# Two-block transformer on one core: last items of the first mixers and stage borders in another order, both tiles' FFN turns in one place, pool means on fewer columns

## The chip, the cores and the metric

The program runs on one core of a Trainium2 chip. Time is the device time of one execution in microseconds (us); lower is better. The engines are named as the profile names them: PE is TensorE (PEld its weight loads), DVE is VectorE, ACT is ScalarE, POOL is GpSimd, SP is SyncE, which here only issues the transfers of weights.

## What is computed

The input x has 256 rows of 1024 columns in float32. Two blocks run one after the other, each of two layers, and each layer is a chain of stages of one form: `x = x + norm(f(norm(x)))`. There are ten stages in all:

```
for l in (0, 1):   # first block
    x = x + rmsnorm(mixer1(rmsnorm(x)))          # four attention kinds, concatenated, @ w_out
    x = x + rmsnorm((silu(h @ w_gate) * (h @ w_up)) @ w_down),  h = rmsnorm(x)
for l in (0, 1):   # second block
    x = x + 0.5 * rms_norm(swiglu(rms_norm(x)))
    x = x + rms_norm(mixer2(rms_norm(x)))        # projections, trailing means, causal convolution, gates
    x = x + 0.5 * rms_norm(swiglu(rms_norm(x)))
```

The inner width of each of the six feed-forward nets (FFN) is 2816. mixer1 has four kinds of attention with four heads of 64 each (moba, fox, mla, dilated), causal within the 256 rows. mixer2 subtracts p from its trailing mean over windows of 2, 4, 8 and 16 rows, one window for each group of 256 columns:

```
def trailing_mean(u, win):
    cs = jnp.cumsum(u, axis=1)
    cs_shift = jnp.pad(cs, ((0, 0), (win, 0), (0, 0)))[:, :s]
    return (cs - cs_shift) / count[None, :, None]     # count = min(row + 1, win)
```

## The kernel before

**Tiles and units.** The rows are two tiles of 128, t = 0 and t = 1. The weights come as units of 128 x 2048 float32 (1 MB) in a fixed row, numbered g. SP loads unit g into one of three buffers `raw`, ACT copies it, rounded to fp32r, into one of four buffers `whi` (two copies of 128x1024, `hi_a` and `hi_b`, L667), and DVE writes the rest `raw - whi` into `wlo` (two halves, `lo`, L1117). A buffer of `whi` comes free when PE has done unit g - 4 for tile 1. `refill(freed)` is the splitting of unit freed + 4. The activations are split the same way (`a_hi`/`a_lo`, `b_hi`/`b_lo`, `f_hi`/`f_lo`). Every product with weights is three matmuls (`three`, L1770 to L1772): high by high, high by low, low by high. One step of PE is one unit for one tile, 12 matmuls of 512 columns; in the FFN row k is step k of tile 0 and then step k - 2 of tile 1.

**Order.** Each engine's order is written out by hand, in loops of Python that are unrolled; the engines meet by semaphores. PE names the sources of waits: `split_done` (weights), `alo` (activations), `fm` (the gated product of the FFN), `o_lo` (a mixer item's heads), `pfree` (a PSUM bank evicted).

**FFN.** In `swiglu` on PE, `gate_up` makes one block j of 256 columns of gate and up, ACT takes the silu (L761), DVE multiplies (L1218, `mult`). `turn_f` (L1825, its transposes L1829) turns the 128x256 product by two PE transposes into `Tp`, ACT and DVE split it into `f_hi` and `f_lo` (L771, L1224), and `down` multiplies it with unit `dn_unit(j)`. There are 11 blocks j for each tile, so 22 pairs of transposes in each FFN.

**First mixer.** It has eight items, M0 to F1 (a kind and a tile). For each: turn q and k (L1945), scores (L1954), mask and maxima on DVE, exponentials on ACT (L871), `turn_p` (L1966), copies of the turned probabilities out of PSUM (`p_out`: the first half by ACT, L882, the second by DVE, L1458), values (L1978), `normalise` (L1471), `turn_heads` (L1984), and `heads_hi`/`heads_lo` (L888, L1479), before `out_part` multiplies the item with its unit of w_out. The last is F1. PE does `turn_p(F1)`, then `out_part(1, OUT_L, L1)`; between the two halves of that (`middle`) stand `values(F1)` and `turn_x_both(0, s+1)`, and behind it `turn_heads(F1)` and `out_part(1, OUT_F, F1)`.

**Borders.** `boundary` on ACT (L732) and DVE (L1185) is what happens between two stages: sums of squares of y (L715), the residual (L1161), x turned by PE (L1785), gained (L1177), and split again (L721, L1182), with three units' splitting in between. It has hooks for work of the first mixer. `first_eviction` is the first work of the next stage. `silu_table` (L755) makes ACT load the table of the silu.

**Start of a first mixer on DVE** (`mixing1`, L1481 on): the latents of tile 0 are normalised, unit b + 4 is split (b is the mixer's first unit; b + 4 is `MV`, the values of moba, which PE takes in `values_chunk`), `rotate_moba` (L1373 to L1382) evicts and rotates q and k, `latents_lo` (L1357, L1359) waits for ACT's copy of the turned latents. In layer 0 the two halves of unit b + 4 stand before `rotate_moba` and behind `latents_lo`, in layer 1 both stand before `rotate_moba`. In layer 1 ACT's `latents_hi` (L837, L839) follows `latents(1, l)` (L829, L832), which waits for the half of unit b + 1 of tile 1.

**Pool means.** `band` holds for each window a 128 x 384 matrix; `pool_means` (L2220 on) multiplies tile 0's rows with its columns 0 to 255 and tile 1's rows with columns 256 to 383, for two column blocks m of each of the four windows.

## Time and profile before

| | us |
|---|---|
| median of 3 runs | 1834.16 (1832.75 to 1835.46) |
| the profiled execution, its own time | 1835.75 |
| its span, first to last instruction | 1834.0 |
| PE busy | 1808.9 (99%) |
| DVE busy | 1110.6 (61%) |
| ACT busy | 911.4 (50%) |
| mean granted clock of PE | 0.998 |

The times of instructions are us from the start of the span. A matmul's duration overlaps the next one's, so the distance from start to start tells what one costs. "[0.93 <-DVE ...]" behind a row is idle time of the engine ahead of that instruction and what ended it. PEclk is the granted clock of TensorE as a share of full speed.

### The profile page before, as it was taken

Reading aid. Unit: us, or ns where it says so; the run is one execution under the profiler, and the core shown is the slowest. Engines: PE = TensorE matmul, PEld = TensorE weight load, DVE = VectorE, ACT = ScalarE, POOL = GpSimd, SP = SyncE. Lnnn points to the kernel's source line nnn. Section 1 sums busy time; section 2 is a strip of 40 time slices with the busy share of each in tenths; the row PEclk is TensorE's granted clock in tenths of the full one; section 3 lists DMA queues with packets and bytes.
Section 4 is the critical chain, followed back from the end, with each engine's and each line's share of the span. In section 5 each row is a group of like instructions: output and inputs, shape, how many; then the busy total and the mean of one; then the engine's idle time right before and its main releaser. Section 6 shows DMA issues by size and latency. Waiting matters only on the chain.

```text
span 1834.0 us, 21875 instructions
## 1 busy us (share of the span) xinstructions
PE 1808.9 (99%) x8663; PEld 1506.9 (82%) x8663; DVE 1110.6 (61%) x1444; ACT 911.4 (50%) x1382; POOL 86.4 (5%) x209
## 2 busy tenths in 40 slices
PE   7999999999999999999999999999999999999998
PEld 6888888888788888888888888888888888888887
DVE  7766655776655575556566765556555666675554
ACT  6555444655544454445455444445444545454443
POOL 4001000200000010001000000001000100010000
PEclk9999999999999999999999999999999999999999
DMA  7434555633455565556555565556555655556552
GB/s 233 138 115 159 185 184 170 197 119 115 162 191 191 190 213 189 184 184 207 168 182 192 170 195 191 188 184 218 184 184 187 208 178 173 195 165 202 184 183 92
DMA packets 221462, 327.80 MB, mean 179 GB/s; under 512 B 10576, under 2 KB 156528, under 8 KB 221104
## 3 DMA queue, kind: packets, MB, share of 16 engines
q1 hardware_dynamic: 218880, 318.64, 53.1%
q0 software_dynamic: 2176, 7.75, 1.4%
q8 instruction: 69, 1.13, 0.3%
q14 instruction: 33, 0.27, 0.0%
q10 hardware_dynamic: 304, 0.01, 0.0%
HBM read 325.31 MB, written 1.05 MB: 178 GB/s over the span
## 4 chain that ended last, share of the span: by engine, by line
PE 96%; ACT 1%; POOL 1%; DVE 1%; issue 1%; DMA 0%; DVEq 0%; POOLq 0%; ACTq 0%
PE Dp L1770 17%; PE Dp L1772 17%; PE Dp L1771 17%; PE Gp L1772 12%; PE Gp L1770 12%; PE Gp L1771 12%; PE Tp L1829 2%; PE Gp L1954 1%; PE Tp L1945 1%; PE Dp L1978 1%; PE Tp L1785 0%; PE Gp L1785 0%; PE Tp L1978 0%; DVE wlo L1117 0%; ACT whi L667 0%
## 5 line engine op out<-in xcount | busy, mean ns | idle before, releaser
L1117 DVE TENSOR_TENSOR wlo<-raw,whi 128x1024 fp32r<-128x1024 f32 (+1 forms) x608 | 715.2, 1214 | 359.2 <-ACT whi L667 359.0
L667 ACT ACTIVATE whi<-raw 128x1024 fp32r<-128x1024 f32 (+1 forms) x608 | 606.5, 1045 | 292.1 <-PE Dp L1772 160.1
L1770 PE MATMUL Gp<-whi,a_hi 128*128 128x512 f32 x960 | 380.1, 396 | 0.0
L1772 PE MATMUL Gp<-whi,a_lo 128*128 128x512 f32 x960 | 374.6, 390 | 0.0
L1771 PE MATMUL Gp<-wlo,a_hi 128*128 128x512 f32 x960 | 373.9, 389 | 0.0
L1770 PE MATMUL Dp<-whi,a_hi 128*128 128x512 f32 (+2 forms) x768 | 294.0, 383 | 4.9 <-DVE wlo L1117 3.2
L1772 PE MATMUL Dp<-whi,a_lo 128*128 128x512 f32 (+2 forms) x768 | 287.9, 375 | 0.0
L1771 PE MATMUL Dp<-wlo,a_hi 128*128 128x512 f32 (+2 forms) x768 | 287.6, 375 | 0.0
L1772 PEld LDWEIGHTS Gp<-whi,a_lo 128*128 128x128 f32 x960 | 180.1, 188 | 38.6
L1771 PEld LDWEIGHTS Gp<-wlo,a_hi 128*128 128x128 f32 x960 | 180.5, 188 | 35.9
L1770 PEld LDWEIGHTS Gp<-whi,a_hi 128*128 128x128 f32 x960 | 180.3, 188 | 35.5
L1770 PE MATMUL Dp<-whi,f_hi 128*128 128x512 f32 x504 | 202.1, 401 | 0.0
L1772 PE MATMUL Dp<-whi,f_lo 128*128 128x512 f32 x504 | 197.7, 392 | 0.0
L1771 PE MATMUL Dp<-wlo,f_hi 128*128 128x512 f32 x504 | 196.5, 390 | 0.0
L1770 PEld LDWEIGHTS Dp<-whi,a_hi 128*128 128x128 f32 x768 | 145.2, 189 | 30.4 <-DVE wlo L1117 4.1
L1772 PEld LDWEIGHTS Dp<-whi,a_lo 128*128 128x128 f32 x768 | 145.0, 189 | 25.5
L1771 PEld LDWEIGHTS Dp<-wlo,a_hi 128*128 128x128 f32 x768 | 145.3, 189 | 23.4
L761 ACT ACTIVATE inner<-Gp,st 128x256 f32<-128x256 f32 x120 | 57.0, 475 | 215.7 <-PE Gp L1772 215.7
L771 ACT ACTIVATE f_hi<-Tp 128x256 fp32r<-128x256 f32 x126 | 48.3, 384 | 189.8 <-PE Tp L1829 189.8
L1218 DVE SCALAR_TENSOR_TENSOR inner<-Gp,st,inner 128x256 f32<-128x256 f32 x120 | 57.7, 481 | 130.5 <-ACT inner L761 130.5
L1224 DVE TENSOR_TENSOR f_lo<-Tp,f_hi 128x256 fp32r<-128x256 f32 x126 | 53.1, 422 | 113.3 <-ACT f_hi L771 113.2
L1772 PEld LDWEIGHTS Dp<-whi,f_lo 128*128 128x128 f32 x504 | 94.6, 188 | 20.6
(261 smaller groups left out, 1649.7 us busy)
## 6 DMA issues: line engine op xcount, KB each, us to landing
raw<-in_ffn_w_gate_up SPq DMA_DIRECT2D x176, 512.0 KB, 4.7
raw<-in_w_in SPq DMA_DIRECT2D x132, 512.0 KB, 4.6
raw<-in_ffn_w_down SPq DMA_DIRECT2D x88, 512.0 KB, 4.4
raw<-in_w_gate SPq DMA_DIRECT2D x44, 512.0 KB, 3.8
raw<-in_w_up SPq DMA_DIRECT2D x44, 512.0 KB, 4.8
raw<-in_w_down SPq DMA_DIRECT2D x44, 512.0 KB, 4.3
raw<-in_w_out SPq DMA_DIRECT2D x16, 512.0 KB, 4.0
raw<-in_w_pool_out SPq DMA_DIRECT2D x16, 512.0 KB, 4.2
```

Source lines behind the costliest of these rows:

```text
L667: return nc.scalar.activation(whi[g % W][0:rows, c0:c0 + n], raw[g % R][0:rows, c0:c0 + n], ACT.Copy).then_inc(hi_done, 1)
L761: nc.scalar.activation(gate[:, t, :], gu_bank(t, j)[:, 0:FC], ACT.Silu, scale=rsx[:, t:t + 1]).then_inc(silu[t], 1)
L771: nc.scalar.activation(f_buf(j, t)[0], T(t, 256).rearrange("p (k s) -> p k s", k=2), ACT.Copy).then_inc(fhi[t], 1)
L1117: return V.tensor_tensor(wlo[g % W][0:rows, c0:c0 + n], raw[g % R][0:rows, c0:c0 + n], whi[g % W][0:rows, c0:c0 + n].bitcast(F32), ALU.sub ...
L1218: V.scalar_tensor_tensor(out=ffn[:, t, :], in0=gu_bank(t, j)[:, FC:2 * FC], scalar=rsx[:, t:t + 1], in1=gate[:, t, :], op0=ALU.mult, op1=A ...
L1224: V.tensor_tensor(lo_, T(t, 256).rearrange("p (k s) -> p k s", k=2), hi_.bitcast(F32), ALU.subtract).then_inc(flo[t], 1)
L1770: mm(o, hi, wh, start=start, stop=False, skip_group_check=True)
L1771: mm(o, hi, wl, start=False, stop=False, skip_group_check=True)
L1772: return mm(o, lo, wh, start=False, stop=stop, skip_group_check=True)
L1829: ins = nc.tensor.transpose(T(t)[:, P * k:P * k + P], ffn[:, t, P * k:P * k + P], ident[:, :])
L1945: ins = nc.tensor.transpose(T(e, 512, dq)[:, P * h:P * h + P], of(kind, t, h), ident[:, :])
L1954: ins = mm(score_view(n)[:, h, :], qT[0:dq, h, :], kT[0:dq, h, 0:nk], start=True, stop=True)
```

## The change

Five edits, all of order but for the last:

1. First mixer, item F1 (both layers): ACT's `p_out(F1)` moves from behind the table load and `refill(last - 2)` to right behind the exponentials. PE's `turn_heads(F1)` moves into `middle`, behind `turn_x_both`. DVE's `heads_lo(F1)` moves between the two `gained` of tile 0.
2. All nine borders: ACT's splitting of unit last + 4 (`refill(last)`) stood behind `first_eviction`; now `hi_a` stands ahead of `turned_hi(1, 0)` and `hi_b` between the two `turned_hi` of tile 1. DVE's part stays.
3. Layer 1's first mixer on DVE: the order of layer 0 is used, so the second half of unit b + 4 moves behind `rotate_moba` and `latents_lo`.
4. FFN: `turn_f(1, j - 1)` moves from its own step to behind `turn_f(0, j)`, ten times in each of six FFNs; ACT's and DVE's splits move with it.
5. Pool means: tile 0's rows are multiplied with the first 128 + window columns of the band (130, 132, 136 and 144) in place of 256.

```
@@ scalar: boundary
                     hi_b(last - 1 + W)
                     square_x(0, s + 1)
+                    if last + W <= LAST:
+                        hi_a(last + W)
                     turned_hi(1, 0, s + 1)
+                    if last + W <= LAST:
+                        hi_b(last + W)
                     turned_hi(1, 1, s + 1)
                     first_eviction()
-                    refill(last)
                     square_x(1, s + 1)
@@ scalar: ffn_step (vector: the same with mult and f_low)
-                elif i == 2:
-                    f_hi_out(t, F, 0)
+                elif (t, i) == (0, 2):
+                    f_hi_out(0, F, 0)
...
-                elif i % 3 == 1 and 4 <= i <= 31:
-                    f_hi_out(t, F, i // 3)
+                elif t == 0 and i % 3 == 1 and 4 <= i <= 31:
+                    f_hi_out(0, F, i // 3)
+                    f_hi_out(1, F, i // 3 - 1)
+                elif (t, i) == (1, NFFN - 2):
+                    f_hi_out(1, F, NJ - 1)
@@ scalar: hooks of mixing1
                     heads_hi(L1, l)
                     softmax(F1, l)
+                    p_out(F1, l)
                     silu_table()
 
                 def after_refill():
-                    p_out(F1, l)
                     heads_hi(F1, l)
@@ vector: boundary
                 if s + 1 < STAGES:
                     gained(0, 0, s + 1)
+                    between_gained()
                     gained(0, 1, s + 1)
@@ vector: mixing1
-                if l:
-                    refill(b + 0)
-                    rotate_moba(0, l)
-                    latents_lo(0, l)
-                else:
-                    lo(b + W, 0)
-                    rotate_moba(0, l)
-                    latents_lo(0, l)
-                    lo(b + W, 1)
+                lo(b + W, 0)
+                rotate_moba(0, l)
+                latents_lo(0, l)
+                lo(b + W, 1)
...
-                def after_gained():
+                def between_gained():
                     heads_lo(F1, l)
@@ tensor: swiglu, step
-                        if i == 2:
-                            turn_f(t, 0)
+                        if (t, i) == (0, 2):
+                            turn_f(0, 0)
...
-                        if (t, i) != (1, NFFN - 2):
-                            turn_f(t, i // 3)
+                        if t == 0:
+                            turn_f(0, i // 3)
+
+                            turn_f(1, i // 3 - 1)
@@ tensor: mixing1
                     turn_x_both(0, s + 1)
 
+                    turn_heads(F1)
+
                 out_part(1, OUT_L, L1, False, False, middle)
-
-                turn_heads(F1)
                 out_part(1, OUT_F, F1, False, True)
@@ tensor: pool_means
-                        mm(bank, rows_of(ZB, 0, c)[:, o:o + P], band[:, g, 0:S], start=True, stop=True)
+                        reach = P + WINDOWS[g]
+                        mm(bank[:, 0:reach], rows_of(ZB, 0, c)[:, o:o + P], band[:, g, 0:reach], start=True, stop=False,
+                           skip_group_check=True)
```

Where the instructions stand now is seen at three places. The lines of code differ by a few between the two kernels: L882, L755 and L721 of before are L888, L758 and L721 of the change. First, ACT at the end of layer 0's first mixer, before (L871 are the exponentials of F1, `loaded2` is the transfer of a unit):

```order
L871 ACTIVATE Z,sm<-Z,sm 128x256 x3
L755 ACT_TABLE_LOAD
L755 ACTIVATE st<-st 128x1
L667 ACTIVATE whi<-raw 128x1024 [waits done1,loaded2]
L667 ACTIVATE whi<-raw 128x1024
L882 ACTIVATE Z<-Gp 128x512 [waits p_turned]
L888 ACTIVATE b_hi<-Gp 128x2x128 [waits o_turned]
L721 ACTIVATE a_hi<-stage 128x4x128 [waits gn0] x2
```

and ACT at the same place in the change:

```order
L877 ACTIVATE Z,sm<-Z,sm 128x256 x3
L888 ACTIVATE Z<-Gp 128x512 [waits p_turned]
L758 ACT_TABLE_LOAD
L758 ACTIVATE st<-st 128x1
L667 ACTIVATE whi<-raw 128x1024 [waits done1,loaded2]
L667 ACTIVATE whi<-raw 128x1024
L894 ACTIVATE b_hi<-Gp 128x2x128 [waits o_turned]
L721 ACTIVATE a_hi<-stage 128x4x128 [waits gn0] x2
```

The copy of the turned probabilities has passed the table load, the dummy silu and the two halves of a unit.

Second, DVE at the start of layer 1's first mixer, before (L1117 are halves of unit b + 4 and then of b + 5, L1338 ends the rotation of the latents' key):

```order
L1338 TENSOR_TENSOR Z<-Z 128x4x16
L1117 TENSOR_TENSOR wlo<-raw,whi 128x1024 [waits hi_done] x2
L1373 SCALAR_TENSOR_TENSOR stage<-Dp,st,sinh 128x512 [waits done0]
L1375 SCALAR_TENSOR_TENSOR Z<-Dp,st,cosh 128x512
L1381 TENSOR_TENSOR Z<-Z,stage 128x8x32 [waits pfree0,rope_m0]
L1382 TENSOR_TENSOR Z<-Z,stage 128x8x32
L1357 TENSOR_TENSOR b_lo<-Tp,b_hi 96x2x128 [waits lhi0]
L1359 TENSOR_TENSOR b_lo<-Tp,b_hi 128x128
L1395 TENSOR_TENSOR st<-Z,bfor 128x8 [waits gmla_in,lat_out1,lat_out0]
```

and DVE there in the change:

```order
L1348 TENSOR_TENSOR Z<-Z 128x4x16
L1123 TENSOR_TENSOR wlo<-raw,whi 128x1024 [waits hi_done]
L1383 SCALAR_TENSOR_TENSOR stage<-Dp,st,sinh 128x512 [waits done0]
L1385 SCALAR_TENSOR_TENSOR Z<-Dp,st,cosh 128x512
L1391 TENSOR_TENSOR Z<-Z,stage 128x8x32 [waits pfree0,rope_m0]
L1392 TENSOR_TENSOR Z<-Z,stage 128x8x32
L1367 TENSOR_TENSOR b_lo<-Tp,b_hi 96x2x128 [waits lhi0]
L1369 TENSOR_TENSOR b_lo<-Tp,b_hi 128x128
L1123 TENSOR_TENSOR wlo<-raw,whi 128x1024 [waits hi_done]
L1405 TENSOR_TENSOR st<-Z,bfor 128x8 [waits gmla_in,lat_out1,lat_out0]
```

The second half of unit b + 4 has moved behind six instructions, two of which wait on ACT's `lhi0`.

Third, PE in a row of the FFN, before, the step `down` of tile 0 with what stands ahead of and behind it (the twelve matmuls of the step are cut to their first and last):

```order
L1829 MATMUL Tp<-ident,inner 128x128 [waits fm1]
L1829 MATMUL Tp<-ident,inner 128x128
L1770 MATMUL Dp<-whi,f_hi 128x512 [waits split_done,flo0]
...
L1772 MATMUL Dp<-whi,f_lo 128x512
L1829 MATMUL Tp<-ident,inner 128x128 [waits fm0]
L1829 MATMUL Tp<-ident,inner 128x128
L1770 MATMUL Gp<-whi,a_hi 128x512 [waits fm1]
```

and PE there in the change:

```order
L1775 MATMUL Dp<-whi,f_hi 128x512 [waits split_done,flo0]
...
L1777 MATMUL Dp<-whi,f_lo 128x512
L1834 MATMUL Tp<-ident,inner 128x128 [waits fm0]
L1834 MATMUL Tp<-ident,inner 128x128
L1834 MATMUL Tp<-ident,inner 128x128 [waits fm1]
L1834 MATMUL Tp<-ident,inner 128x128
L1775 MATMUL Gp<-whi,a_hi 128x512 [waits fm1]
```

Tile 1's pair of transposes has moved one step later and stands behind tile 0's.

## Rows read from the trace of the kernel before

**Rows 1.** The page, busy time of each engine and its share of the span.
```profile
PE 1808.9 (99%) x8663; PEld 1506.9 (82%) x8663; DVE 1110.6 (61%) x1444; ACT 911.4 (50%) x1382; POOL 86.4 (5%) x209
```

**Rows 2.** Waits of PE, the largest in the body: us in total, times, longest.
```profile
PE Tp L1978 <- ACT Z L882: 2.8, 2, 1.4
```

**Rows 3.** Timeline, end of layer 0's first mixer: start, duration, instruction.
```profile
132.71 1.28 ACT L755 ACT_TABLE_LOAD   x1
133.87 0.69 DVE L1458 COPY Z<-Gp 128x512 f32<-128x512 f32 x1 [0.95 <-PE Gp L1966]
134.11 1.99 ACT L667 ACTIVATE whi<-raw 128x1024 fp32r<-128x1024 f32 x2
134.83 0.40 PE L1772 MATMUL Dp<-whi,b_lo 128*128 128x512 f32 x1
136.63 2.00 PE L1978 MATMUL Tp<-Z 128*128 128x64 f32 x16 [1.41 <-ACT Z L882]
...
142.76 0.38 ACT L888 ACTIVATE b_hi<-Gp 128x256 fp32r<-128x256 f32 x1 [6.18 <-PE Gp L1984]
143.65 0.50 PE L1770 MATMUL Dp<-whi,b_hi 128*128 128x512 f32 x1 [0.93 <-DVE b_lo L1479]
```

**Rows 4.** Stretches: length, busy PE, PEld, DVE, ACT, POOL, PEclk, DMA.
```profile
135.30:138.70 3.40, 2.07 (x19) 2.07 (x20) 0.03 (x1) 1.28 (x2) 0.00 (x0) 1.00 0.00 0
138.70:142.10 3.40, 3.40 (x13) 2.92 (x12) 1.77 (x3) 0.00 (x0) 0.00 (x0) 0.50 0.00 0
456.10:459.50 3.40, 3.40 (x14) 3.03 (x14) 1.81 (x3) 0.00 (x0) 0.00 (x0) 0.50 0.00 0
96.40:98.13 1.73, 1.73 (x17) 1.73 (x16) 0.44 (x3) 1.47 (x2) 0.00 (x0) 1.00 1.02 407
123.30:126.70 3.40, 3.40 (x25) 3.19 (x24) 2.07 (x2) 2.00 (x2) 0.00 (x0) 1.00 0.35 121
```

**Rows 5.** Timeline of PE, steady step and a pair of transposes (501.53), layer 1's FFN.
```profile
501.30 0.39 PE L1772 MATMUL Dp<-whi,f_lo 128*128 128x512 f32 x1
...
504.29 0.39 PE L1772 MATMUL Gp<-whi,a_lo 128*128 128x512 f32 x1
...
508.60 0.39 PE L1770 MATMUL Gp<-whi,a_hi 128*128 128x512 f32 x1
...
510.87 0.39 PE L1771 MATMUL Gp<-wlo,a_hi 128*128 128x512 f32 x1
```

**Rows 6.** Timeline of PE around four transposes in a run (L1966 at 47.46).
```profile
47.23 0.39 PE L1772 MATMUL Dp<-whi,a_lo 128*128 128x512 f32 x1
...
50.44 0.40 PE L1772 MATMUL Dp<-whi,a_lo 128*128 128x512 f32 x1
```

**Rows 7.** Timeline of PE in the pool means, first window, layer 0.
```profile
872.23 0.60 PE L2229 MATMUL Tp<-band,Z 128*128 128x256 f32 x2
872.67 0.38 PE L2230 MATMUL Tp<-band,Z 128*128 128x128 f32 x2
872.89 0.60 PE L2229 MATMUL Tp<-band,Z 128*128 128x256 f32 x2
```

**Rows 8.** Timeline, border into layer 1's first mixer and its start.
```profile
340.76 0.63 ACT L721 ACTIVATE a_hi<-stage 128x512 fp32r<-128x512 f32 x1 [1.10 <-DVE stage L1177]
343.61 2.36 DVE L1117 TENSOR_TENSOR wlo<-raw,whi 128x1024 fp32r<-128x1024 f32 x2 [1.49 <-ACT whi L667]
344.89 0.50 PE L1770 MATMUL Dp<-whi,a_hi 128*128 128x512 f32 x1 [1.08 <-DVE wlo L1117]
349.69 0.38 PE L1929 MATMUL Tp<-ident,Z 128*96 128x128 f32 x2
350.81 0.39 PE L1770 MATMUL Dp<-whi,a_hi 128*128 128x256 f32 x1 [0.63 <-DVE Z L1375]
352.09 0.28 DVE L1359 TENSOR_TENSOR b_lo<-Tp,b_hi 128x128 fp32r<-128x128 f32 x1
353.77 1.03 PE L1945 MATMUL Tp<-ident,Z 128*64 128x128 f32 x8
```

More of the change, by code:

```diff
@@ L1183, in turned_lo, with boundary @@
                                 ).then_inc(alo[t], 1)
-            def boundary(s, last, after_scaled, after_residual, after_gained, first_eviction):
+            def boundary(s, last, after_scaled, after_residual, between_gained, after_gained, first_eviction):
                 scaled(0, 0, s)
@@ L1229, in ffn_step @@
                     mult(t, F, 0)
-                elif i == 2:
-                    f_low(t, F, 0)
+                elif (t, i) == (0, 2):
+                    f_low(0, F, 0)
                 elif i % 3 == 0 and 3 <= i <= 30:
                     mult(t, F, i // 3)
-                elif i % 3 == 1 and 4 <= i <= 31:
-                    f_low(t, F, i // 3)
+                elif t == 0 and i % 3 == 1 and 4 <= i <= 31:
+                    f_low(0, F, i // 3)
+                    f_low(1, F, i // 3 - 1)
+                elif (t, i) == (1, NFFN - 2):
+                    f_low(1, F, NJ - 1)
             def swiglu(F, g0, between=None):
@@ L1248, in end_of_ffn @@
             def end_of_ffn(s, F, g0, first_eviction):
-                boundary(s, g0 + NFFN - 1, nothing, lambda: ffn_step(1, F, NFFN - 3),
+                boundary(s, g0 + NFFN - 1, nothing, lambda: ffn_step(1, F, NFFN - 3), nothing,
                          lambda: ffn_step(1, F, NFFN - 2), first_eviction)
@@ L1581, in after_residual @@
                     normalise(F1, l)
-                def after_gained():
+                def between_gained():
                     heads_lo(F1, l)
-                return after_scaled, after_residual, after_gained
+                return after_scaled, after_residual, between_gained, nothing
             def v_eviction(t, c, l):
@@ L1760, in _ @@
                 g0 = mixer2(l) + 37
-                boundary(s_mix2(l), g0 - 1, nothing, nothing, nothing, lambda: mult(0, f_22(l), 0))
+                boundary(s_mix2(l), g0 - 1, nothing, nothing, nothing, nothing, lambda: mult(0, f_22(l), 0))
                 swiglu(f_22(l), g0)
```

## The prediction

> **What bounds the kernel.** The page first: PE is busy 1808.9 of 1834.0 us, no other engine over 61% [rows 1]. So the time is PE's own work, plus its idle time (25 us, part of it in the start-up, which the change leaves alone), plus what the granted clock takes. A change of order can win only (a) a wait of PE, (b) a stretch at half clock, (c) the small losses at the seams between kinds of matmul; taking columns away wins (d) their streaming time.
>
> The waits of PE come next. The largest in the body is that of `values(F1)` for ACT's copy: 2.8 us in two waits, one for each layer of the first mixer [rows 2]. The timeline shows what stands there [rows 3]: PE has its last matmul at 134.83 and could go on at 135.06 (matmuls start 0.227 us apart: 2.27 for ten, 508.60 to 510.87 [rows 5]). It starts at 136.63, because ACT first loads a table (1.28) and splits a unit (1.99). Then comes a stretch in which PE is busy with only 2.07 of 3.40 us, and behind it the granted clock is 0.50 from 138.7 to 142.1, and in the same way from 456.1 to 459.5 in the other layer [rows 4]; 0.50 is the lower of TensorE's two levels, 1.2 GHz. Last, PE waits 0.93 for DVE's `heads_lo(F1)` at 143.65.
>
> **Edit 1, item F1.** The copy needs turned probabilities and a free ACT. ACT is free at 132.71; DVE does the other half of the same copy from 133.87 to 134.56 with its order unchanged [rows 3], and ACT's half is released earlier, by the first four transposes. So both halves are done by 134.56, ahead of PE's 135.06: the wait goes whole. From there at full clock: 16 value products 1.73 (96.40 to 98.13 [rows 4]); ten transposes, eight of x and the two of `turn_heads(F1)` that now stand here, at 0.11 each, 1.10 (0.11: see edit 4); the second half of `out_part(L1)`, six matmuls 1.36, and 0.13 for the seam. 135.06 + 1.73 + 1.10 + 1.36 + 0.13 = 139.4 for the first matmul of `out_part(F1)`, where before had 143.65: **4.3 us**. Of this 1.6 is the first wait and up to 1.7 the half clock (3.40 us at half rate do the work of 1.70), and the rest is the wait at 143.65, which is hidden now: the heads' transposes start at 137.7 and are out by 138.3, and from the start of ACT's `heads_hi` to PE it took 0.89 (142.76 to 143.65), so 139.2, with 0.2 in hand. ACT is free for it at 134.1 + 1.28 + 1.99 = 137.4. What is late next: DVE's `gained(0, 1)` now waits behind `heads_lo(F1)`, which moves the border's chain (split, residual, gained) some 0.3 to 0.5 us closer to PE. Ahead of `turn_f(0, 0)` there is almost nothing in hand, so I allow 0.1 of new wait. Two layers: 2 x 4.3 = 8.6, less 0.1.
>
> Bounds: if the clock still falls in both layers, 8.6 - 3.4 = 5.2; if the border gives back 0.5 each, 7.6.
>
> A rule of the skill speaks against the whole of this. The Trainium skill, TensorE: Matmul & The Clock Gate, Part 4, says that PE transposes do not count as busy in the same way as matmuls for the clock; the edit puts ten of them behind 16 small products, 2.8 us without one large matmul. By that rule the clock might fall as before, and the sum would be 3.4 less; by the row the stretch 123.3 to 126.7 is all small products, PE busy throughout, and keeps 1.00. I follow the row, and keep the fall as a rival.
>
> **Edit 2, the borders.** `hi_b` of unit last + 4 goes into a gap of ACT that is 1.10 long (340.76 [rows 8]) and takes 0.99 to 1.05 (half of 1.99 [rows 3]); `hi_a` goes into a longer one ahead. It fits with some 0.05 to spare, so no `turned_hi` comes later: 0. If it did not fit, the first block's product would be late by what is missing. The one gain is at the border into layer 1's mixer: PE's wait of 1.08 for the split of that unit (344.89), with the tail of the matmul before it 1.24, goes, since DVE need not wait for ACT (its 1.49 of idle time at 343.61).
>
> **Edit 3, start of layer 1's mixer.** With `rotate_moba` one half (1.2) and edit 2's gain earlier, the wait of 0.63 at 350.81 (0.8 with the tail) goes as well: 2.0 together. But the second half of unit b + 4 is now behind `latents_lo`, and `values_chunk` needs it after 12 of its 24 matmuls. In before, `latents_lo` ended at 352.37, 2.68 behind the start of the turned latents (349.69), a chain over ACT that follows PE. 349.69 moves to 348.45; `latents_lo` ends at 351.13, the half at 351.13 + 1.18 = 352.3, where PE wants it at 348.8 + 1.5 = 350.3. The new wait is 2.0 and PE goes on at 352.3 with 12 matmuls, 1.5: 353.8 for the next item, where before had 353.77 [rows 8]. **Edits 2 and 3 together: 0**; what the border gives, the moved half takes back. Bounds: -2 (if the half were early) to +0.5.
>
> **Edit 4, the turns.** A pair alone: from 501.30 to 504.29 there are twelve steps of 0.227 (2.72) and the pair, so it costs 0.27 [rows 5]. Four in a run: 47.23 to 50.44 is 3.21, so 0.49 [rows 6]; the two added cost 0.22, 0.11 each. Two pairs apart cost 0.54, together 0.49: 0.05 saved. Ten in each of six FFNs: 60 x 0.05 = **3.0 us**. No engine waits newly: tile 1's split has four steps (11 us) before its `down`. Bounds: 0 if the seam's loss comes once for each bank rather than for each run, 4 by the rounding of the rows (0.01 on each).
>
> **Edit 5, pool means.** Two instructions of 256 columns take 0.44 (872.23 to 872.67), two of 128 take 0.22 (to 872.89) [rows 7]: 0.86 ns a column and instruction. The columns fall by 126, 124, 120 and 112, 482 in sum, in two instructions for each of two blocks and two layers: 482 x 8 x 0.86 ns = **3.3 us**. Bounds: 3.0 to 3.4, since 128 columns already run at the rate of 256.
>
> **Sum.** 8.5 + 0 + 3.0 + 3.3 = 14.8 us. Against the profiled execution's own time: 1835.75 - 14.8 = 1820.9. The median of the runs is 1.6 under that execution and the lowest 3.0; an execution of before that did not fall to half clock would be about 3 lower, and of the change none should fall. So I read the sum from the profiled time, and lean 0.4 toward the median: **1820.5**. A difference of 0.2% (3.7 us) is about what a measurement of this kernel tells from none.
>
> **Rivals.**
> - Half clock stays in both layers: for it the rule above, against it the stretch at 123.3. Then 14.8 - 3.4 = 11.4, 1824 (in one layer, 1822.5). Chance 0.14.
> - The seam's loss is per bank, edit 4 gives nothing: 14.8 - 3.0 = 11.8, 1823.5. For it: the four in rows 6 write one bank, the new four write two. Chance 0.12.
> - Layer 1's half comes early enough or late with more: 1819, or 1822. Chance 0.08.
> - Only the waits that a row names move, and reordering gives back the rest at the border (as for edits 2 and 3, also for edit 1): the columns and half the turns are left, under 5 us, 1830. The change does not do what it says. Chance 0.04.
> - Slower: at the nine borders ACT now stands in `hi_a(last + 4)` before `turned_hi(1, 0)`. If the unit's transfer has not landed, ACT waits, the turned x of tile 1 waits behind it, then the first silu, then PE. It decides from 14.8 / 9 = 1.65 us of wait in each border. Against it: the `whi` that the rows show at this place (134.11) waited for no transfer. At 2 us each it would be 1839. Chance 0.03.
> - The forecast, 1818.5 to 1822.5 by the bounds of edits 1, 4 and 5: 0.59.
>
> The range takes in all but the last two and the far end of the first, where both the clock falls and the turns give nothing (14.8 - 6.4 = 8.4, 1827): 1817 to 1825. Faster by over 0.2%: 0.94; same 0.03; slower 0.03.
>
> The changes of sign come from the last rival (slower) and from half of the one before it with more given back (same).
>
> **What the profile of the changed kernel should show.** No wait of PE at L1978's counterpart, the first `out_part(F1)` matmul near 139.4; no slice with PEclk 0.50 in the two mixers (edit 1 right); a wait of about 2 us of PE for DVE's `wlo` in layer 1's `values_chunk`, inside a run of 256-column matmuls (edit 3 right), none at 344.89's counterpart (edit 2); each FFN shorter by 0.5, no wait of PE in it; the pool means of a window at 0.9 us in place of 1.3. I would be wrong if a new wait stood at each border, or if the stretch behind F1 still ran at 0.50.

## The result, and the profile after

| | before | after |
|---|---|---|
| median, us (lowest to highest) | 1834.81 (1832.75 to 1836.18) | 1820.52 (1820.10 to 1820.59) |
| ratio, 95% interval | | 0.9923 [0.9911, 0.9935] |
| profiled execution, its own time | 1835.75 | 1820.46 |
| its span | 1834.0 | 1818.7 |

The change is faster by 14.3 us in the medians and by 15.3 in the two profiled executions. The forecast was 14.8 against the profiled one and 1820.5 for the time.

The busy line of the page, after. It answers to [rows 1].

```profile
PE 1800.1 (99%) x8663; PEld 1506.4 (83%) x8663; DVE 1103.8 (61%) x1444; ACT 912.9 (50%) x1382; POOL 95.7 (5%) x209
```

PE is busy 8.8 us less, and idle 6.5 us less (18.6, before 25.1). The instruction counts are the same. POOL's are the same instructions too, and take 9.3 us more in all (95.7, before 86.4): in every profile with edit 2 POOL is busy 95.7 to 96.7 us, in every one without it 85.7 to 87.0. Why is not shown; behind the start-up PE waits for POOL nowhere. The waits of PE, after, largest first:

```profile
PE Dp L1775 <- DVE wlo L1123: 3.9, 3, 2.0
...
PE Dp L1775 <- DVE a_lo L1188: 0.9, 1, 0.9
PE Tp L1943 <- DVE st L1419: 0.8, 1, 0.8
PE Dp L1961 <- DVE Z L1431: 0.4, 1, 0.4
PE Tp L1952 <- DVE b_lo L1369: 0.3, 1, 0.3
```

The wait for ACT's copy of F1's probabilities [rows 2] is gone. Of the first row, two waits of 2.2 together lie in the start-up, where before has them too; 1.65 is new. Line numbers have moved: `three` is now L1775 to L1777, `values` L1985, ACT's copy L888.

The timeline at the end of layer 0's first mixer answers to [rows 3].

```profile
133.58 0.60 ACT L888 ACTIVATE Z<-Gp 128x512 f32<-128x512 f32 x1 [0.75 <-PE Gp L1973]
134.02 0.69 DVE L1468 COPY Z<-Gp 128x512 f32<-128x512 f32 x1 [0.95 <-PE Gp L1973]
134.20 1.28 ACT L758 ACT_TABLE_LOAD   x1
134.97 0.40 PE L1777 MATMUL Dp<-whi,b_lo 128*128 128x512 f32 x1
135.21 1.89 PE L1985 MATMUL Tp<-Z 128*128 128x64 f32 x16
135.60 1.99 ACT L667 ACTIVATE whi<-raw 128x1024 fp32r<-128x1024 f32 x2
137.82 0.38 PE L1991 MATMUL Gp<-ident,inner 128*128 128x128 f32 x2
138.24 0.38 ACT L894 ACTIVATE b_hi<-Gp 128x256 fp32r<-128x256 f32 x1 [0.65 <-PE Gp L1991]
138.66 0.42 DVE L1489 TENSOR_TENSOR b_lo<-Gp,b_hi 128x256 fp32r<-128x256 f32 x1 [0.38 <-ACT b_hi L894]
139.43 0.40 PE L1775 MATMUL Dp<-whi,b_hi 128*128 128x512 f32 x1
```

Read it by PE: no row of PE has a bracket, so it has no idle time. ACT's copy is done at 134.18 and DVE's at 134.71, PE takes them at 135.21. `out_part(F1)` starts at 139.43, 4.46 us behind the last matmul of the first half (134.97); in before the same two were 8.82 apart (134.83 and 143.65 [rows 3]). DVE's `b_lo` ends at 139.08, 0.35 ahead of PE.

The stretches that answer to [rows 4], and one in the start-up:

```profile
26.58:29.99 3.41, 3.34 (x8) 2.66 (x9) 2.49 (x9) 2.12 (x8) 2.88 (x6) 0.50 0.72 112
137.00:140.41 3.41, 3.41 (x22) 2.97 (x22) 2.77 (x6) 2.20 (x5) 0.00 (x0) 1.00 0.00 0
450.00:453.41 3.41, 3.41 (x21) 2.93 (x20) 2.91 (x6) 2.19 (x5) 0.00 (x0) 1.00 0.00 0
```

Behind F1 the clock keeps 1.00 in both layers. In this execution it fell once in the start-up, at 26.58, at the end of a wait of 1.97 (PE goes on at 26.65); before has this wait too (1.87), without a fall.

Layer 1's start, DVE and PE, answers to [rows 8]:

```profile
343.81 0.27 PE L1937 MATMUL Tp<-ident,Z 128*128 128x128 f32 x1
344.12 0.38 PE L1775 MATMUL Dp<-whi,a_hi 128*128 128x256 f32 x1
...
346.00 0.28 DVE L1369 TENSOR_TENSOR b_lo<-Tp,b_hi 128x128 fp32r<-128x128 f32 x1
346.19 1.21 DVE L1123 TENSOR_TENSOR wlo<-raw,whi 128x1024 fp32r<-128x1024 f32 x1
...
347.46 0.39 PE L1775 MATMUL Dp<-whi,a_hi 128*128 128x256 f32 x1 [1.65 <-DVE wlo L1123]
349.00 0.27 PE L1952 MATMUL Tp<-ident,Z 128*64 128x128 f32 x1
```

`values_chunk` starts at 344.12 without a bracket. It is not quite free of the rotation: it starts 0.31 behind the transpose ahead of it, where in e9 below, in which the rotation is long done, the same two are 0.02 apart. It then stands still in its middle until the second half of unit b + 4, split from 346.19 on, is done.

Four transposes in a run in an FFN of layer 1 (x4 in one row), then the block of a window's pool means:

```profile
491.90 0.39 PE L1777 MATMUL Dp<-whi,f_lo 128*128 128x512 f32 x1
492.13 0.60 PE L1834 MATMUL Tp<-ident,inner 128*128 128x128 f32 x4
...
495.08 0.39 PE L1777 MATMUL Gp<-whi,a_lo 128*128 128x512 f32 x1
...
861.93 0.39 PE L2237 MATMUL Tp<-band,Z 128*128 128x130 f32 x2
862.16 0.38 PE L2239 MATMUL Tp<-band,Z 128*128 128x128 f32 x2
862.38 0.39 PE L2237 MATMUL Tp<-band,Z 128*128 128x130 f32 x2
```

From 491.90 to 495.08 are 3.18 us: twelve steps of 0.227 and 0.46 for the four. One block of the means takes 0.45 (861.93 to 862.38), before 0.66 [rows 7].

To see where the 15.3 us come from, the same matmul (counted from the start) is looked up in both timelines:

| stretch | before | after | less by |
|---|---|---|---|
| start to the last matmul ahead of values(F1), layer 0 | 134.83 | 134.97 | -0.14 |
| from there to the first matmul behind turn_f(0, 0) | 20.92 | 16.62 | 4.30 |
| on to the border into layer 1's mixer (one FFN) | 184.43 | 183.84 | 0.59 |
| border and start of layer 1, to the next 512-column matmul behind turn_qk(M0) | 14.38 | 14.36 | 0.02 |
| to the last item of layer 1 | 97.69 | 97.69 | 0.00 |
| item F1 of layer 1, with its border | 21.16 | 16.83 | 4.33 |
| the two second mixers | 428.80 | 425.57 | 3.23 |
| the other five FFNs | | | 2.95 |

### The profile page after: what moved, and what is told of

Same layout as the page of the kernel before. It is cut to its first block, busy times and chain, and to the rows that moved or that the text cites. A ratio compares the mean times of both kernels' runs of the same rounds, so it can differ in the third digit from the quotient of the medians.

```text
span 1818.7 us, 21875 instructions
## 1 busy us (share of the span) xinstructions
PE 1800.1 (99%) x8663; PEld 1506.4 (83%) x8663; DVE 1103.8 (61%) x1444; ACT 912.9 (50%) x1382; POOL 95.7 (5%) x209
## 4 chain that ended last, share of the span: by engine, by line
PE 97%; POOL 1%; DVE 1%; issue 0%; ACT 0%; DMA 0%; DVEq 0%; POOLq 0%; ACTq 0%
PE Dp L1775 18%; PE Dp L1777 18%; PE Dp L1776 18%; PE Gp L1775 12%; PE Gp L1777 12%; PE Gp L1776 12%; PE Tp L1834 2%; PE Gp L1961 1%; PE Tp L1952 1%; PE Dp L1985 1%; PE Tp L1790 0%; PE Gp L1973 0%; PE Gp L1790 0%; PE Tp L1985 0%; PE Dp L1961 0%
## 5 line engine op out<-in xcount | busy, mean ns | idle before, releaser
L1775 PE MATMUL Gp<-whi,a_hi 128*128 128x512 f32 x960 | 379.6, 395 | 0.0
L1777 PE MATMUL Gp<-whi,a_lo 128*128 128x512 f32 x960 | 374.3, 390 | 0.0
L1775 PE MATMUL Dp<-whi,a_hi 128*128 128x512 f32 (+2 forms) x768 | 294.9, 384 | 5.0 <-DVE wlo L1123 3.9
L1777 PE MATMUL Dp<-whi,a_lo 128*128 128x512 f32 (+2 forms) x768 | 288.6, 376 | 0.0
L1777 PEld LDWEIGHTS Gp<-whi,a_lo 128*128 128x128 f32 x960 | 180.2, 188 | 38.6
L1775 PEld LDWEIGHTS Gp<-whi,a_hi 128*128 128x128 f32 x960 | 180.3, 188 | 35.4
L1775 PE MATMUL Dp<-whi,f_hi 128*128 128x512 f32 x504 | 196.6, 390 | 0.0
L1777 PE MATMUL Dp<-whi,f_lo 128*128 128x512 f32 x504 | 196.4, 390 | 0.0
L1775 PEld LDWEIGHTS Dp<-whi,a_hi 128*128 128x128 f32 x768 | 145.6, 190 | 30.4 <-DVE wlo L1123 4.7
L1777 PEld LDWEIGHTS Dp<-whi,a_lo 128*128 128x128 f32 x768 | 145.4, 189 | 25.9
L1777 PEld LDWEIGHTS Dp<-whi,f_lo 128*128 128x128 f32 x504 | 94.6, 188 | 19.7
L1775 PEld LDWEIGHTS Dp<-whi,f_hi 128*128 128x128 f32 x504 | 94.6, 188 | 19.5
L1776 PEld LDWEIGHTS Dp<-wlo,f_hi 128*128 128x128 f32 x504 | 94.6, 188 | 19.4
```

The source lines that it names most:

```text
L1775: mm(o, hi, wh, start=start, stop=False, skip_group_check=True)
L1776: mm(o, hi, wl, start=False, stop=False, skip_group_check=True)
L1777: return mm(o, lo, wh, start=False, stop=stop, skip_group_check=True)
```

## Experiments

e1, e2, e3, e8 and e9 start from the kernel before and are set against its profile in the same stretches; e4, e5, e6 and e10 start from the changed kernel and are set against that, e7 against e4 and e11 against e7. The ratios are those to the kernel before, timed beside each (medians 1834.5 to 1835.5).

### e1: edit 1 alone

```diff
                     softmax(F1, l)
+                    p_out(F1, l)
                     silu_table()
...
                     turn_x_both(0, s + 1)
+                    turn_heads(F1)
                 out_part(1, OUT_L, L1, False, False, middle)
-                turn_heads(F1)
```

(and DVE's `heads_lo(F1)` between the two `gained`, as in the change)

> The kernel before with edit 1 alone (item F1 of both first mixers). My account: it is worth 4.3 us in each layer, 8.6 us in all, ratio 0.9953, and the profile shows no PE wait ahead of values(F1), the first matmul of out_part(F1) at about 139.4 and a granted clock of 1.00 behind it in both layers. Rival A: the clock falls anyway when the other edits are absent: 5.2 us, ratio 0.9972. Rival B: edit 1 needs edit 2 (ACT's splitting moved at the border), so that the border gives back over 1 us in each layer ahead of the first turn of the FFN: 6 to 7 us, ratio 0.9965.

Measured: 1827.20 us, ratio 0.9959 [0.9947, 0.9972]. The stretches of e1 at the places of F1:

```profile
137.00:140.41 3.41, 3.41 (x20) 2.91 (x19) 2.91 (x6) 2.20 (x5) 0.00 (x0) 1.00 0.00 0
450.00:453.41 3.41, 3.41 (x22) 2.99 (x21) 2.81 (x6) 2.19 (x5) 0.00 (x0) 1.00 0.00 0
```

The first matmul of `out_part(F1)` starts at 139.05. In the profile the two layers give 4.31 and 4.33, 8.6 in all. The timed runs say 7.5 (5.1 to 9.7 by the interval). That this is less than 8.6 is most likely because not every execution of before falls to half clock in both layers (below); only one execution of it has a trace. Edit 1 stands alone. It is the profile that settles the rivals: the clock does not fall (A), and the border behind the item is as long as in the change (B); the interval of the timed runs alone would take in B and just reach A.

### e2: edit 4 alone

```diff
-                        if (t, i) != (1, NFFN - 2):
-                            turn_f(t, i // 3)
+                        if t == 0:
+                            turn_f(0, i // 3)
+                            turn_f(1, i // 3 - 1)
```

(with the same move of `f_hi_out` on ACT and `f_low` on DVE)

> The kernel before with edit 4 alone (60 pairs of FFN transposes joined to runs of four). My account: what is lost at a seam comes once for each run of transposes, so each joined pair saves 0.05 to 0.06 us, 3.0 to 3.5 us in all, each FFN about 0.55 us shorter, ratio 0.9982. Rival: the loss comes once for each PSUM bank, 0 us, ratio 1.000, each FFN as long as before (187.2 us from one border's turn to the next).

Measured: 1830.86 us, ratio 0.9981 [0.9972, 0.9990]. From layer 0's border to the end its profile gains 3.56 us on that of before, about 0.6 in each of the six FFNs; the first mixer of layer 1 gains 0.05. The stretch is taken from the border on because in this profile the clock did not fall at item F1 of layer 0 (1.58 us less there, with the program of before). The rival of a loss for each bank is out.

### e3: edit 5 alone

```diff
-                        mm(bank, rows_of(ZB, 0, c)[:, o:o + P], band[:, g, 0:S], start=True, stop=True)
+                        reach = P + WINDOWS[g]
+                        mm(bank[:, 0:reach], rows_of(ZB, 0, c)[:, o:o + P], band[:, g, 0:reach], start=True, stop=False,
+                           skip_group_check=True)
```

> The kernel before with edit 5 alone (pool means on the columns that are reached). My account: 3856 columns of a step of 0.86 ns, 3.3 us, ratio 0.9982, each second mixer 1.65 us shorter and the rest of the program as before. Rival: shorter matmuls (130 to 144 columns) cost as much as those of 256 because their weight loads (128x128) set the pace: 0 us, ratio 1.000.

Measured: 1831.56 us, ratio 0.9981 [0.9973, 0.9990]. The two second mixers are shorter by 1.64 and 1.61 us, 3.25 in all; the rival (matmuls of 130 to 144 columns cost as much as those of 256) falls. The profile of e3 shows something else beside it, at the two places of item F1, where the program is that of before:

```profile
136.60:140.01 3.41, 3.41 (x28) 3.28 (x29) 1.37 (x3) 0.00 (x0) 0.00 (x0) 1.00 0.00 0
453.58:460.41 6.83, 6.64 (x26) 5.55 (x25) 1.81 (x3) 0.15 (x1) 0.00 (x0) 0.50 0.00 0
```

In layer 0 PE waited its 1.4 us for ACT's copy, and the clock did not fall; in layer 1 it fell for 6.8 us instead of 3.4. So the wait makes a fall possible, and not certain. What a fall costs can be read here: from the last matmul ahead of the wait to the first of `out_part(F1)`, layer 0 took 8.82 us in before with it and 7.22 in e3 without it, 1.60.

### e4: the changed kernel, second half of unit b + 4 inside the rotation

The half stands between the two parts of `rotate_moba` in layer 1: `rotate` calls what it is given behind its two `scalar_tensor_tensor`, the second of which frees the bank in PSUM.

```diff
                 lo(b + W, 0)
-                rotate_moba(0, l)
-                latents_lo(0, l)
-                lo(b + W, 1)
+                if l:
+                    rotate_moba(0, l, lambda: lo(b + W, 1))
+                    latents_lo(0, l)
+                else:
+                    rotate_moba(0, l)
+                    latents_lo(0, l)
+                    lo(b + W, 1)
```

> The changed kernel with one more reordering in layer 1's first mixer: DVE splits the second half of unit b + 4 between the two halves of rotate_moba (behind the eviction of the product, ahead of the sums), not behind latents_lo. My account: the 1.66 us wait of PE for that half (347.46 in the profile of the changed kernel) goes whole, since the half is done at 345.3 and PE wants it at 345.6, and the rotation (346.1) and the latents (346.8) are still ahead of turn_qk(M0) at 347.1: 1.7 us below the changed kernel, 1818.8 us, ratio 0.9914. Rival: the wait moves to turn_qk(M0), which now stands behind a later rotation and later latents, and gives back 0.5 to 1 us: 1819.5 or above.

Measured: 1818.10 us, ratio 0.9910 [0.9897, 0.9924]. DVE in e4:

```profile
342.56 0.74 DVE L1385 SCALAR_TENSOR_TENSOR Z<-Dp,st,cosh 128x512 f32<-128x512 f32 x1
343.22 1.21 DVE L1123 TENSOR_TENSOR wlo<-raw,whi 128x1024 fp32r<-128x1024 f32 x1
...
345.36 0.28 DVE L1369 TENSOR_TENSOR b_lo<-Tp,b_hi 128x128 fp32r<-128x128 f32 x1
```

DVE never waits here; the half is done at 344.43, and PE does not stop in the middle of `values_chunk` any more, nor at turn_qk(M0); the start of `values_chunk` is still 0.38 behind the transpose ahead of it (0.31 in the change). The stretch is 1.9 us shorter than in the changed kernel: the whole wait (1.65, 1.82 from start to start) and a little more. Its rival falls.

### e5: the changed kernel, ACT's copy late again

```diff
                     softmax(F1, l)
-                    p_out(F1, l)
                     silu_table()
...
                 def after_refill():
+                    p_out(F1, l)
                     heads_hi(F1, l)
```

> The changed kernel with ACT's copy of F1's turned probabilities put back behind the table load and the split (only that step of edit 1 undone, in both layers). PE waits about 1.6 us ahead of values(F1) again. Theory A: what lets the clock fall is this idle time with small products behind it, so the granted clock is 0.50 for 3.4 us or more behind layer 1's F1 again, and can be in layer 0: 3.2 us of waits and 1.7 to 3.4 us of clock, 1825.4 to 1827.1. Rival B: the clock fell for the second wait (0.93, DVE's heads_lo) or for the order of the small products, which stay as changed: clock 1.00 in both mixers, 3.2 us, 1823.7.

Measured: 1824.30 us, ratio 0.9940 [0.9923, 0.9956]. Its wait (first fence), and the stretches behind it in layer 0, and around and behind it in layer 1 (second):

```profile
PE Tp L1985 <- ACT Z L888: 2.8, 2, 1.4
```

```profile
138.42:141.83 3.41, 3.41 (x15) 3.12 (x14) 1.99 (x4) 0.90 (x2) 0.00 (x0) 0.50 0.00 0
449.00:452.41 3.41, 2.00 (x12) 1.40 (x10) 0.69 (x1) 3.17 (x5) 0.00 (x0) 1.00 0.33 110
452.50:455.91 3.41, 3.41 (x30) 3.27 (x30) 1.24 (x3) 0.55 (x2) 0.00 (x0) 1.00 0.00 0
```

The clock fell in layer 0 and not in layer 1. Set against the change, item F1 up to its `out_part` costs 3.28 us more in layer 0 and 1.67 more in layer 1: 1.67 for the wait alone, 1.61 for the fall. The border behind it gives 0.23 of layer 0's back, so 3.06 and 1.68 are left. Theory A holds in kind (with the wait the fall is back, rival B is out), though it was layer 1 that I had counted on. The median, 1824.3, lies between the two figures. The profiled execution took 1824.8, below A's lowest figure of 1825.4 even with its one fall, because of the 0.23 that the border gives back and a start-up that was 0.3 shorter than the change's. The other three have no trace.

### e6: the changed kernel, turn_heads(F1) late again

```diff
                     turn_x_both(0, s + 1)
-                    turn_heads(F1)
                 out_part(1, OUT_L, L1, False, False, middle)
+                turn_heads(F1)
                 out_part(1, OUT_F, F1, False, True)
```

> The changed kernel with turn_heads(F1) on PE back behind the second half of out_part(L1), and the early copy kept (only that step of edit 1 undone, both layers). PE then waits about 1 us for DVE's heads_lo(F1) ahead of out_part(F1), whose first matmul comes at about 139.9 instead of 139.4. Theory A: no idle time ahead of values(F1), so no fall: clock 1.00, 0.4 to 1 us in each layer, 1821.3 to 1822.5. Rival B: a wait of 1 us beside the small products is enough for the fall: 1.7 us more in each layer that falls, 1823 to 1825.9.

Measured: 1823.23 us, ratio 0.9937 [0.9923, 0.9952]. The wait, and the two stretches around it in layer 0:

```profile
PE Dp L1775 <- DVE b_lo L1489: 1.9, 2, 0.9
```

```profile
138.00:141.41 3.41, 3.41 (x27) 3.08 (x26) 1.12 (x2) 1.63 (x2) 0.00 (x0) 1.00 0.00 0
141.41:144.82 3.41, 2.48 (x12) 1.85 (x11) 2.64 (x5) 2.58 (x5) 0.00 (x0) 1.00 0.00 0
```

The wait of 0.93 is back in both layers and the clock stays at 1.00: theory A on the clock, against rival B. Two places would be weak evidence alone, since a fall is not certain behind the longer wait either; the profile of before adds that its falls at F1 start at 138.7 and 456.1, ahead of its waits of 0.93 at 143.65 and 461.31. The cost is 1.09 us to the first matmul of `out_part(F1)`, 0.12 in its first two matmuls and 0.19 at the border, 1.4 in each layer and 2.8 in all, more than the 0.8 to 2 that I had expected.

### e7: e4, and layer 0's start in another order

```diff
-                lo(b + W, 0)
                 if l:
+                    lo(b + W, 0)
                     rotate_moba(0, l, lambda: lo(b + W, 1))
                     latents_lo(0, l)
+                    forget_a(l)
+                    refill(b + 1)
+                    k_turned(M0, l)
                 else:
                     rotate_moba(0, l)
                     latents_lo(0, l)
-                    lo(b + W, 1)
-                forget_a(l)
-                refill(b + 1)
-                k_turned(M0, l)
+                    refill(b + 0)
+                    k_turned(M0, l)
+                    forget_a(l)
+                    refill(b + 1)
```

> The kernel of run e4 with one more reordering, at the start of layer 0's mixer on DVE: rotate_moba and latents_lo stand ahead of both halves of unit b + 4, and k_turned(M0) ahead of forget_a and the splitting of unit b + 5. My account: the rotation ends at 31.5 and the latents at 32.1, so PE's wait of 1.85 at 33.81 and that of 0.37 at 38.09 go, and the halves (33.3 and 34.5) are there when values_chunk wants them: 2.2 us below e4, 1815.9, ratio 0.9898. Rival: the start-up is tied to later waits (0.85 at 43.01 on the forget gates' chain over ACT), which take it back: 0 to 0.5 us, 1818.

Measured: 1818.49 us (1816.21 to 1819.95), ratio 0.9908 [0.9894, 0.9923]. In its profile (the execution of 1816.21) the waits of 1.85 and 0.37 are gone, 2.0 us against e4 from 28 to 37 us; at the next one 0.4 comes back (in e4 it was 0.86):

```profile
PE Tp L1951 <- DVE st L1420: 1.3, 1, 1.3
```

So 1.6 us is won in the profile, 2.2 expected; in the medians nothing (by the ratios, 0.9908 and 0.9910, 0.4 us, far inside the interval). The four executions have mean clocks of 1.000, 0.999, 0.999 and 0.998, and the slower ones are those with the lower clock. The changed kernel shows why that may matter here: the matmul that started at 28.67 in before started there at 30.36, behind its fall in the start-up, but the one of 39.80 at 39.92, since the wait for `b_lo` in between was 0.3 instead of 1.85. Without that wait a fall in the start-up would count in full. That reading of e7's other three executions, which have no trace, is argued and not shown.

### e8: edit 2 alone

```diff
                     square_x(0, s + 1)
+                    if last + W <= LAST:
+                        hi_a(last + W)
                     turned_hi(1, 0, s + 1)
+                    if last + W <= LAST:
+                        hi_b(last + W)
                     turned_hi(1, 1, s + 1)
                     first_eviction()
-                    refill(last)
```

> The kernel before with edit 2 alone (ACT's halves of unit last + 4 moved ahead of turned_hi at nine borders). In its profile PE's wait of 1.08 us at the border into layer 1's mixer is gone, 1.24 us with the tail; the wait of 0.63 that follows (for rotate_moba) grows to 0.9, since DVE reaches it only 1.0 us earlier; net 1.0 us less in that stretch, and nothing at the eight other borders. Rival: turned_hi(1, 0) comes late at the other borders, PE waits there ahead of the FFN, up to 0.5 us each, 4 us slower in all.

Measured: 1834.33 us, one execution. In its profile the wait at the border is gone (1.25 us), the next one has grown from 0.63 to 1.17:

```profile
PE Dp L1773 <- DVE Z L1378: 1.2, 1, 1.2
```

Net 0.8, 1.0 expected. At the other borders the difference to before moves by less than 0.05 us: no wait there, the rival is out.

### e9: edit 3 alone

```diff
-                if l:
-                    refill(b + 0)
-                    rotate_moba(0, l)
-                    latents_lo(0, l)
-                else:
-                    lo(b + W, 0)
-                    rotate_moba(0, l)
-                    latents_lo(0, l)
-                    lo(b + W, 1)
+                lo(b + W, 0)
+                rotate_moba(0, l)
+                latents_lo(0, l)
+                lo(b + W, 1)
```

> The kernel before with edit 3 alone (second half of unit b + 4 behind latents_lo in layer 1, the border as before). My account: the wait of 0.63 for the rotation goes, and a wait of 1.7 to 2.0 for the half comes 1.5 us later in the same values_chunk; the next item starts 0.8 to 1.1 us later than in before, the time is 1 us longer. Rival: the half is early without edit 2, because PE comes 1.2 us later: no new wait, 0.8 us less.

Measured: 1838.02 us, one execution; in the profile 2.8 us longer from the border to the next item. Its wait (timeline of PE), and the stretch behind it:

```profile
353.05 0.58 PE L1765 MATMUL Dp<-whi,a_hi 128*128 128x256 f32 x1 [1.94 <-DVE wlo L1117]
```

```profile
353.06:356.47 3.41, 3.41 (x16) 3.28 (x17) 2.45 (x4) 0.50 (x2) 0.00 (x0) 0.50 0.57 141
```

The wait is 1.94, as expected; with it the stretch would be 1.3 us longer (1.94 and 0.2 of tail, less the 0.8 of the wait that is gone). The other 1.5 us is a fall of the clock that I had not thought of. It starts where PE goes on after the wait. The changed kernel has the same wait a little shorter (1.65) and kept 1.00 there, as did e5 and e6.

### e10: the changed kernel without edit 3

The diff of e9 the other way round, on the changed kernel.

> The changed kernel with edit 3 undone (in layer 1 both halves of unit b + 4 ahead of rotate_moba). By run e8, where this order stands with edit 2, PE waits 1.17 us once for the rotation and not 1.66 for the half: 0.8 us less in that stretch than the changed kernel, so 1819.7, ratio 0.9918. Rival: the two edits need each other, so the undone one costs what edit 2 brought, 1.2 us more: 1821.7.

Measured: 1819.61 us, ratio 0.9915 [0.9900, 0.9930]; in the profile the stretch is 0.66 us shorter than in the change, with one wait in it:

```profile
PE Dp L1780 <- DVE Z L1385: 1.3, 1, 1.3
```

So edit 3, as part of the change, costs 0.7 us. The difference in the medians, 0.9, is well below the 3.7 us that a measurement can tell from none; it agrees, and the trace decides. The rival falls.

### e11: e7, and forget_c ahead of the mask

```diff
+                forget_c(l)
                 mask(M0, l)
                 maxima(M0, l)
-                forget_c(l)
```

> The kernel of run e7 with one more step moved on DVE in both first mixers: forget_c ahead of mask(M0) and maxima(M0), since its input from ACT is there at 39.75 in e7. My account: PE's wait of 1.25 at 41.48 goes; the next thing that PE can wait for is the softmax of M0 (44.6 in e7, which doesn't move), so 0.6 to 0.7 us of the 1.25 are kept: 0.65 us below e7 for the same clock, 1815.6 in an execution that never falls to half clock, 1817.5 with one fall at the start. Rival: the softmax comes later by the 0.35 that mask and maxima are moved back, and turn_p(M0) takes back all: as e7, or slower by 0.3.

Measured: 1815.77 us (1815.49 to 1816.02), ratio 0.9895 [0.9879, 0.9912], the fastest kernel of the study, 4.75 us below the change. The wait of 1.3 for the forget gates is replaced by the one for M0's softmax:

```profile
PE Tp L1981 <- ACT Z L877: 0.6, 1, 0.6
```

Against e7 it gains 0.5 us in this stretch (0.65 expected), and 0.26 ahead of it, in the start-up, where the program is that of e7 and x landed earlier (PE's longest wait for it is 2.7, in e7 3.0). In layer 1 the same move gains nothing (that stretch is 0.08 longer). All four executions have a mean clock of 1.000, so what a fall in the start-up would cost it was not seen.

## Why the prediction was right

- **Edit 1.** Forecast 8.5 for both layers, measured 8.6 (4.30 and 4.33, and the same in e1). The three parts are confirmed one by one, each to the first matmul of `out_part(F1)`: the first wait 1.67 (e5, layer 1; forecast 1.6), the half clock 1.61 (e5 and e3, layer 0; up to 1.7), the wait for `heads_lo` 1.09 (e6; 1.0 left over in the forecast). Together they are 4.37, and from the last matmul of the first half to this one the change is 4.37 shorter (8.82 and 4.46). The border was allowed to give back 0.05 in each layer and gives back 0.06, but as a difference of two things that the forecast had not seen: behind the wait of 0.93, before lost 0.12 in its first two matmuls, which the change does not, and in the change the first turn of the FFN costs 0.19 more. `turn_f(0, 0)` starts at 151.39, though PE's steps of 0.227 would have it there at 151.26, since DVE's product for it, now later, ends at 151.34.

```profile
150.86 0.48 DVE L1225 SCALAR_TENSOR_TENSOR inner<-Dp,st,inner 128x256 f32<-128x256 f32 x1
151.03 0.39 PE L1777 MATMUL Gp<-whi,a_lo 128*128 128x512 f32 x1
151.39 0.44 PE L1834 MATMUL Tp<-ident,inner 128*128 128x128 f32 x2
```

- **Edits 2 and 3.** Forecast 0, measured 0.02, and both halves of the bargain are near where I put them. The border gives 1.25 (forecast 1.24) and 0.1 more, since the first matmul behind a wait is slow and that wait is gone. The rotation gives 0.6 (forecast 0.8): the distance from the last transpose to `values_chunk` shrinks from 0.90 to 0.31, and its wait does not go whole. PE stands 1.82 us in `values_chunk` (345.64 to 347.46; forecast 2.0), again with 0.1 in the first matmul behind it. 1.94 is gained and 1.92 lost. What the forecast did not say is that the wait at the rotation would first grow, to 1.17, once PE comes earlier (e8); so edit 2 is worth 0.8 alone and edit 3 costs 0.7 to 0.8 beside it. The zero is a sum of two numbers that could have been had apart.
- **Edit 4.** Forecast 3.0, measured 3.5: 0.059 for each of 60 pairs instead of 0.05. The term was mis-sized by the rounding of two rows. Averages over all seams of their kind say it better: 0.268 us for a pair (126 seams in before) and 0.480 for four (59 seams after), 2 x 0.268 - 0.480 = 0.056.
- **Edit 5.** Forecast 3.3, measured 3.2.
- **The clock.** The rival that it falls anyway did not happen. The Trainium skill, TensorE: Matmul & The Clock Gate, Part 4, says that PE transposes do not count as busy in the way matmuls do. In the changed kernel ten transposes stand behind 16 small products in both layers and the granted clock is 1.00, and no other run here shows a fall behind transposes without a wait ahead of them. The forecast was right on this with a poor reason: the stretch 123.3 to 126.7 that it followed holds score and value products and not one transpose, so it could not speak to that rule. Rows of before that could are the 16 transposes in a run from 91.90 on, behind matmuls of 256 columns; the clock is 1.00 there.

```profile
91.90 1.03 PE L1966 MATMUL Gp<-ident,Z 128*128 128x128 f32 x8
92.77 1.04 PE L1945 MATMUL Tp<-ident,Z 128*66 128x128 f32 x8
...
123.29 1.89 PE L1954 MATMUL Gp<-Z 66*128 66x256 f32 x8
125.02 1.90 PE L1978 MATMUL Tp<-Z 128*128 128x64 f32 x16
```

  One sign of the forecast failed: it said that no slice in the two mixers would show 0.50, and that no execution of the change should fall. The fall at 26.58 lies in layer 0's mixer, in its start-up, which the forecast took as left alone; three of the four executions of the change have a mean clock of 0.998. It cost nothing there (last section).
- **The sum.** 14.8 forecast, 15.3 between the two profiles, of which the missing 0.5 is edit 4. That 1820.5 was met to 0.02 us is luck. The sum alone gave 1820.9; the 0.4 taken off it toward the median of before has no ground in the result, since the change's median (1820.52) and its profiled execution (1820.46) agree, and it happened to make up for what edit 4 was put too low. The median gain is 14.3, below the 15.3 of the profiles, because the median of before lies under its profiled execution. That executions of before differ in how often the clock falls is the likely reason. Of the 21 that were timed beside e1 to e4, the four with a mean clock of 0.999 took 1832.6 to 1833.5 us, while the 15 with 0.997 took 1834.0 to 1835.8 (the two with 0.998 took 1832.5 and 1835.7).

## What to carry to other kernels

A short wait of the bottleneck engine costs more than its length when it can drop the clock behind it: in item F1 1.4 us of idle time cost 1.7 directly and 1.6 more when the clock fell. Before moving work behind another step, ask who wants it in the middle of a step, not only at its start: unit b + 4 was needed after half of `values_chunk`, and its second half fitted between the eviction and the sums of the rotation (e4), a place that neither of the two written orders used. And when an edit's parts sum to nothing, take them apart: here one was worth 0.8 us and the other cost as much.

## What was not expected of the hardware

At one and the same place of the program the granted clock falls in some executions and not in others. Counted over the 13 profiled executions of this case: at item F1, where PE had waited 1.4 us ahead of the small products (before, e2, e3, e5, e8, e9, two layers each), the clock fell in 9 of 12 places; where it had not waited (the change, e1, e4, e6, e7, e10, e11), in 0 of 14. Behind the wait of 1.6 to 1.9 us in layer 1's `values_chunk` it fell in 1 of 4 (e9). In the start-up it fell behind the wait of 1.6 to 2.1 us at about 26.5 in 4 of 12 (the change, e2, e3, e10) and behind one of 2.44 in e6, and behind the wait of 1.8 to 1.9 us at about 34 in none of six. Taken together from 15 us on: PE has 35 waits of 1.40 to 2.44 us in the 13 profiles, and behind 15 of them the clock fell, from 0.1 us ahead of the end of the wait to 2.2 us behind it; behind 32 waits of 0.83 to 1.27 us it never did, and no fall came without a wait of 1.40 or more (but for the one behind the last matmul of each execution). So the length of the wait alone doesn't decide. Falls last 3.4 us, once 6.8, and each 3.4 us cost 1.4 to 1.6 where nothing behind it took that in. What decides within a place whether it falls was not settled; no run here takes that apart.

A fall can also be free. In the start-up of the change's profile it cost 1.56 us at first (30.36 against 28.67, where the two stood 0.13 apart ahead of it), and the wait for DVE behind it took all of that in.
